# Experts' input rows transposed by VectorE from gathered quarter rows; three waits of the experts' stage moved

## What is computed

```
def swiglu(t, wg, wu, wd):
    return (jax.nn.silu(t @ wg) * (t @ wu)) @ wd

def moe_swiglu(h, router_w, wg, wu, wd):
    ...
    logits = (t @ router_w).astype(jnp.float32)
    top_logits, top_idx = lax.top_k(logits, TOP_K)
    top_w = jax.nn.softmax(top_logits, axis=-1)
    gates = jnp.einsum('tk,tke->te', top_w, jax.nn.one_hot(top_idx, N_EXPERTS, dtype=jnp.float32)).astype(h.dtype)
    y = jnp.zeros_like(t)
    for e in range(N_EXPERTS):
        y = y + gates[:, e:e + 1] * swiglu(t, wg[e], wu[e], wd[e])
    return y.reshape(bsz, s, d)
```

## Time and profile before

| | us |
|---|---|
| median of 3 executions | 1933.41 |
| lowest, highest | 1933.14, 1934.14 |
| the profiled execution's own time | 1928.41 |
| its span, first to last instruction | 1926.7 |

### The profile page before, as it was taken

One profiled execution on the slowest core, in us unless ns is written; L12 is line 12 of the kernel. 1 busy time (PEld: TensorE's weight loads), 2 busy tenths in 40 slices (PEclk: granted clock), 3 DMA queues, 4 the chain that ended last, 5 costly groups with the idle time before them and its releaser, 6 DMA issues. The chain is left out here.

```text
span 1926.7 us, 36862 instructions
## 1 busy us (share of the span) xinstructions
PE 1888.7 (98%) x15078; PEld 1624.8 (84%) x15078; DVE 924.8 (48%) x1225; ACT 578.5 (30%) x1234; POOL 723.9 (38%) x624
## 2 busy tenths in 40 slices
PE   9999999999999999999999999999999999999997
PEld 8778744888887888888877888778999999999996
DVE  3898687667565455444436788865200000000023
ACT  1443213555533111110036657533120211111102
POOL 5755523565544334344526777652200000000011
PEclk9999999999999999999999999999999999999999
DMA  9213750222215666631211111102957578778893
GB/s 336 88 56 143 263 210 34 78 93 88 83 44 202 212 204 213 218 121 61 104 66 67 68 58 69 65 13 83 325 203 251 196 233 275 253 265 333 335 351 152
DMA packets 82824, 313.58 MB, mean 163 GB/s; under 512 B 10121, under 2 KB 10641, under 8 KB 82529
## 3 DMA queue, kind: packets, MB, share of 16 engines
q1 hardware_dynamic: 75952, 289.73, 42.5%
q0 software_dynamic: 4464, 14.35, 2.2%
q10 hardware_dynamic: 2241, 7.14, 1.0%
HBM read 301.43 MB, written 9.75 MB: 162 GB/s over the span
## 5 line engine op out<-in xcount | busy, mean ns | idle before, releaser
L261 PE MATMUL banks<-sb_act,sb_ring 128*64 128x112 f32 (+9 forms) x5088 | 621.0, 300 | 1.1 <-ACT sb_ring L468 0.7
L261 PEld LDWEIGHTS banks<-sb_act,sb_ring 128*128 128x128 f32 (+1 forms) x5088 | 592.5, 174 | 23.1 <-issue 4.5
L261 PE MATMUL banks<-sb_x_norm,sb_ring 128*128 128x256 f32 (+3 forms) x1616 | 330.9, 403 | 3.4 <-ACT sb_ring L468 2.3
L261 PEld LDWEIGHTS banks<-sb_x_norm,sb_ring 128*128 128x128 f32 (+1 forms) x1616 | 242.3, 171 | 66.5 <-issue 29.3
L3732 DVE TENSOR_TENSOR sb_act<-sb_work,banks 128x192 f32<-128x192 f32 (+7 forms) x88 | 27.2, 309 | 482.8 <-PE banks L261 475.2
L443 POOL TENSOR_TENSOR sb_ring<-sb_ring 128x512 f32<-128x512 f32 x146 | 205.1, 1405 | 102.0 <-PE banks L261 53.9
L261 PE MATMUL banks<-sb_work,sb_ring 128*64 128x256 f32 (+2 forms) x1124 | 231.6, 407 | 3.9 <-ACT sb_ring L468 2.7
L261 PEld LDWEIGHTS banks<-sb_work,sb_ring 128*128 128x128 f32 (+1 forms) x1124 | 155.9, 165 | 57.7 <-issue 35.3
L3263 POOL DMA_INDIRECT sb_work<-first_expert_rows,sb_table x8 | 7.5, 939 | 442.6 <-DMA first_expert_rows<-sb_x_norm 440.4
L3534 ACT ACTIVATE sb_work<-banks 128x192 f32<-128x192 f32 (+7 forms) x88 | 25.8, 294 | 295.2 <-PE banks L261 293.2
L2370 ACT ACTIVATE sb_work<-banks 128x256 f32<-128x256 f32 x84 | 32.3, 384 | 216.8 <-PE banks L261 216.8
(11 more groups left out here) (530 smaller groups left out, 2588.8 us busy)
## 6 DMA issues: line engine op xcount, KB each, us to landing
sb_ring<-in_w_moe_up SPq DMA_DIRECT2D x176, 512.0 KB, 4.9
sb_ring<-in_w_moe_down SPq DMA_DIRECT2D x64, 704.0 KB, 6.4
sb_act<-in_cond_w SPq DMA_DIRECT2D x84, 512.0 KB, 3.7
sb_ring<-in_w_ffn_up SPq DMA_DIRECT2D x44, 512.0 KB, 5.2
sb_ring<-in_w_h_in SPq DMA_DIRECT2D x32, 512.0 KB, 4.2
sb_ring<-in_w_in SPq DMA_DIRECT2D x28, 512.0 KB, 5.9
sb_ring<-in_w_m_in SPq DMA_DIRECT2D x24, 512.0 KB, 3.9
sb_ring<-in_w_ffn_down SPq DMA_DIRECT2D x16, 704.0 KB, 5.4
```

The source lines that it names most:

```text
L261: last = m.nc.tensor.matmul(out[part], weights[:, part], act, start=start, stop=stop, skip_group_check=skip)
```

## The change

- Rows in DRAM lie in quarters: `normed_rows` has 2048 rows of 256 values instead of 512 of 1024. A quarter row q holds 32 features of each of the eight blocks of 128. ACT no longer stores them. POOL copies `x_rows` into that order (`quartered`, in `HN` and `more`) after its scatters, once the first gated product of rank 0 is there (`m.evac` at `done + 2`), and stores the copies itself, once weight block 7 of rank 0 has landed.
- The scattered numbers are four times the token. POOL reads them four times, once for each group of 32 partitions, and adds the quarter's number (three small instructions).
- A tile is gathered by four indirect DMAs with 128 quarter rows each: 36 in place of 9.
- DVE transposes a tile with four instructions of 32x32 blocks straight into `xT`, behind the last gated product of a rank. PE's `turn` is gone. ACT's `take_turned` scales and shifts within `xT`.
- `turn_result` stands at the start of the downward blocks of ranks 1 to 5 and no more ahead of block 4, and so does ACT's `take_result`.
- PE starts the downward blocks when ten of the eleven gated blocks are there and waits for the last ahead of its eleventh product.
- ACT waits in rank 0 until the rows are stored, ahead of its copies of the downward blocks.

```diff
self.small = sb("small", [P, 64])
-        self.table = sb("table", [P, 3 * ST + GATHERS + 1 + EXPERTS + 4 * ST], U32)
+        self.table = sb("table", [P, 3 * ST + 1 + EXPERTS + 4 * ST], U32)
+        self.row_parts = sb("row_parts", [P, 4 * GATHERS], U32)
         self.rank_caps = sb("rank_caps", [P, EXPERTS])
...
         self.d_tokens = dram("tokens_of_expert", (PASSES * ROWS, 1), U32)
-        self.d_rows = dram("normed_rows", (S, D))
+        self.d_rows = dram("normed_rows", (4 * S, DG))
         self.d_first = dram("first_expert_rows", (FIRST[-1] + ROWS - sum(CAPS), D))
...
     per_pass = EXPERTS * total
-    over_at = 3 * ST + GATHERS
+    over_at = 3 * ST
     too_many = m.table[0:1, over_at:over_at + 1]
-    token_rows = m.table[:, 3 * ST:3 * ST + GATHERS]
-    tokens = m.d_tokens.rearrange("(p t q) o -> p q (t o)", t=GATHERS, q=P)
+    tokens = m.d_tokens.rearrange("(p g q) o -> p q (g o)", g=4 * GATHERS, q=QUARTER)
+    by_quarter = lambda t: t.rearrange("p (q k c) -> p k q c", q=4, c=QUARTER)
+    stored_rows = m.d_rows.rearrange("(t q) c -> t (q c)", q=4)
+    quartered = [t.rearrange("p a c -> p (a c)") for t in (m.HN[:, 0:2, :], m.HN[:, 2:4, :], m.HN[:, 4:6, :], m.more[:])]
+    row_parted = m.sem("r_row_parted")
     order = m.sem("e_order")
...
                         m.table[:, 2 * ST + t:2 * ST + t + 1], None).then_inc(scattered, 16)
+            pool.wait_ge(m.evac, done + 2)
+            for t in range(ST):
+                pool.wait_ge(row_out, t + 1)
+                give(pool, nc.gpsimd.tensor_copy(by_quarter(quartered[t]), x_rows[:, t, :].rearrange(
+                    "p (k q c) -> p k q c", q=4, c=QUARTER)), row_parted, t + 1)
+            pool.wait_ge(m.loaded[SLOTS - 1], 16 * (uses[SLOTS - 1] + 1))
+            for t in range(ST):
+                pool.dma_start(stored_rows[rows(t, P), :], quartered[t]).then_inc(row_stored, 16)
             pool.wait_ge(scattered, 16 * 2 * ST)
...
                     pool.sem_inc(order, 1)
-                pool.dma_start(token_rows, tokens[p], allow_slow_non_contiguous=True).then_inc(idx_in, 16)
-                pool.wait_ge(idx_in, p * 16 + 16)
+                for q in range(4):
+                    pool.dma_start(m.row_parts[rows(q, QUARTER), :], tokens[p],
+                                   allow_slow_non_contiguous=True).then_inc(idx_in, 16)
+                pool.wait_ge(idx_in, p * 64 + 64)
                 pool.sem_inc(order, 1)
+                for q in range(1, 4):
+                    part = m.row_parts[rows(q, QUARTER), :]
+                    m.glink.on(pool)(nc.gpsimd.tensor_scalar(part, part, q, None, ALU.add))
                 for i in range(first_pass(p), GATHERS):
...
                         pool.sem_inc(order, 1)
-                    nc.gpsimd.indirect_dma_start(
-                        got[i % BUFS], None, m.d_rows,
-                        bass.IndirectOffsetOnAxis(ap=token_rows[:, i:i + 1], axis=0)
-                    ).then_inc(got_sem[i % BUFS], 16)
+                    for q in range(4):
+                        c = 4 * i + q
+                        nc.gpsimd.indirect_dma_start(
+                            got[i % BUFS][:, rows(q, DG)], None, m.d_rows,
+                            bass.IndirectOffsetOnAxis(ap=m.row_parts[:, c:c + 1], axis=0)
+                        ).then_inc(got_sem[i % BUFS], 16)
                 if not first_pass(p):
...
 
-                def turn(i):
-                    pe.wait_ge(got_sem[i % BUFS], p * (16 * got_used[i % BUFS]) + 16 * (
-                        i // BUFS + (i % BUFS > 0) + (not first_pass(p))))
-                    if not first_pass(p) or i >= 3:
-                        pe.wait_ge(turned_out, p * GATHERS + (i - 2))
-                    for k in range(KD):
-                        last = nc.tensor.transpose(ps[:, 4 + 2 * (i % 2) + k // 4, rows(k % 4, P)],
-                                                   got[i % BUFS][:, rows(k, P)], m.c("ident"))
-                    last.then_inc(turned, 1)
-
                 def turn_result(r):
                     pe.wait_ge(m.evac, p * per_pass + (r * total + done + total))
-                    pe.wait_ge(turned_out, p * GATHERS + (need[min(r + 1, EXPERTS - 1)] - 1))
                     for k in range(KD):
...
                     pe.sem_inc(order, 1)
-                    for i in range(need[0]):
-                        turn(i)
                 for r in range(EXPERTS):
...
                         s = b % SLOTS
-                        if b == 4 and 0 < r <= turned_ranks:
-                            turn_result(r - 1)
                         if closing and b >= up:
...
                         if b == up:
+                            if 1 < r <= turned_ranks + 1:
+                                pe.wait_ge(y_copied, p * copies + copies_until(r - 2))
+                                pe.sem_inc(order, 1)
                             if 0 < r <= turned_ranks:
-                                pe.wait_ge(y_copied, p * copies + copies_until(r - 1))
-                                pe.sem_inc(order, 1)
-                            for i in tiles_beside(p, r):
-                                turn(i)
-                            pe.wait_ge(m.evac, p * per_pass + (base + up))
+                                turn_result(r - 1)
+                            pe.wait_ge(m.evac, p * per_pass + (base + up - 2))
                             pe.sem_inc(order, 1)
...
                                 pe.wait_ge(x0_out, max(x0_first, k) + 1)
+                            if b == up and k == KE - 1:
+                                pe.wait_ge(m.evac, p * per_pass + (base + up))
+                                pe.sem_inc(order, 1)
                             if closing and b > up and k == kt // 2:
...
                                                scale=norm.inv[:, t:t + 1]), row_out, t + 1)
-                act.dma_start(m.d_rows[rows(t, P), :], x_rows[:, t, :]).then_inc(row_stored, 16)
             for k in range(KD):
...
                     act.wait_ge(turned, p * GATHERS + i)
-                    pair = 4 + 2 * (i % 2)
                     for k in range(KD):
-                        last = nc.scalar.activation(xT[:, k, rows(i, P)], ps[:, pair + k // 4, rows(k % 4, P)],
-                                                    ACT.Identity, bias=norm.shift(k), scale=norm.scale(k))
+                        x = xT[:, k, rows(i, P)]
+                        last = nc.scalar.activation(x, x, ACT.Identity, bias=norm.shift(k), scale=norm.scale(k))
                     last.then_inc(turned_out, 1)
...
                     for j in range(KE):
-                        if j == 2 and 0 < r <= turned_ranks:
-                            take_result(r - 1)
                         if j == 2 and closing:
...
                                              ACT.Silu).then_inc(silu, 1)
+                    if 0 < r <= turned_ranks:
+                        take_result(r - 1)
                     for i in tiles_beside(p, r):
                         take_turned(i)
+                    if first_pass(p) and r == 0:
+                        act.wait_ge(row_stored, 16 * ST)
                     if closing:
...
             step(nc.vector.tensor_copy(m.table[:, over_at:over_at + 1], most))
-            step(nc.vector.tensor_copy(m.table[:, 2 * ST:3 * ST], m.c("tok_id")))
+            step(nc.vector.tensor_scalar(m.table[:, 2 * ST:3 * ST], m.c("tok_id"), 4.0, None, ALU.mult))
             give(dve, nc.vector.tensor_copy(m.table[:, 0:2 * ST], m.small[:, 3 * ST:5 * ST]), tables, 1)
...
                 for i in (2 * t, 2 * t + 1):
-                    dve.wait_ge(got_sem[i], 16 * ((1 if turn == 1 else PASSES) * got_used[i] - (i == 0) + turn))
+                    dve.wait_ge(got_sem[i], 64 * ((1 if turn == 1 else PASSES) * got_used[i] - (i == 0)) + 16 * turn)
                 a1, a2 = got[2 * t], got[2 * t + 1]
...
 
+            def turn(p, i):
+                dve.wait_ge(got_sem[i % BUFS], p * (64 * got_used[i % BUFS]) + 64 * (
+                    i // BUFS + (i % BUFS > 0) + (not first_pass(p))))
+                for q in range(4):
+                    at = i * P + q * QUARTER
+                    last = nc.vector.transpose(xT[:, :, at:at + QUARTER], got[i % BUFS][:, rows(q, DG)])
+                last.then_inc(turned, 1)
+
             def body(p):
+                if not first_pass(p):
+                    for i in range(need[0]):
+                        turn(p, i)
                 for r in range(EXPERTS):
...
                             mix(j - 4, 1)
+                    for i in tiles_beside(p, r):
+                        turn(p, i)
                     if closing:
...
```

## The result

The changed kernel takes 1956.55 us (median of four, 1954.78 to 1957.73) against 1933.38 (1933.14 to 1934.14) of the kernel before: a ratio of 1.0118, 95% interval 1.0106 to 1.0130. It is **slower** by 23 us; the forecast was 1925.3, faster by 8. In the profiled executions the spans are 1954.1 and 1926.7 us, 27.4 apart.

What follows compares the result with a forecast made beforehand. It took PE to bound the experts' stage, with DMA engines the second limit. Terms -8.15 - 0.3 + 0.3 = -8.15 us gave 1925.3 us; range 1922.8 to 1932.5.

Steps and rivals of the forecast that it cites:

- The step that failed: POOL's queue behind tile 2: the other gathers (36 in all, 45 us) are wanted only in rank 1's downward part; cost 0.
- Transposes off PE: Experts' stage: 72 transposes of gathered tiles leave PE, all on the path; gain 8.15 us.
- VectorE's transposes: Beside downward parts: four DVE transposes a tile, 0.42 us each, hidden while DVE waits for PE; time 0.
- The waits around the downward product: Start after ten of eleven gated blocks: gain 0.3 us in rank 7, cost 0.3 for waits already met.
- Results turned later, ACT in rank 5: Downward part: ACT's first copy needs 8.7 us, four blocks take 9.6; cost 0, upper end 1 us.
- GpSimd's chain: Rank 0: copies, stores, token reads, additions, gathers on POOL; tile 2 lands at 1412, due 1415; cost 0.
- the first rival: Tile 2 lands 1 to 12 us late, PE stands at rank 0's fifth downward block; 1929.3 with 4 us; chance 0.17.
- the doubled chain: Rank 0: slow token reads, copies and landing on GpSimd stall PE by 16 us, 1941 us; chance 0.10.
- GpSimd's wait for the first gate: Rank 0: POOL's copies start only when the first gate ends at 1358.6; no cost of its own.
- the third rival: Ranks 5 to 7: weight loads become the limit as PE asks sooner; half the gain lost, 1929.4 us; chance 0.08.
- The carry to the median: Whole kernel: the profiled execution's 5.0 us under the median was taken to carry over, 1920.3 becoming 1925.3 us.

Runs made afterwards that it cites:

- experiment 9: The repaired kernel, but PE again waits for all eleven gated blocks ahead of a downward part: 1924.56 us, ratio 0.9961.
- the repaired kernel: Changed kernel; GpSimd waits until each tile's four gathers land, rank 7's eight gathers come in two groups of four: 1919.88 us, ratio 0.9936.
- experiment 10: The repaired kernel without GpSimd's wait for the first gated product ahead of its four copies: 1925.46 us, ratio 0.9960.
- experiment 1: Changed kernel with the gathers of tiles 3 to 8 waiting, one tile each, behind every second gated product of rank 1: 1924.68 us.

## Why the prediction was wrong

- **The step that failed** stands at the end of the part on GpSimd's rows: "Queued behind it ... on POOL the other gathers (36 in all, 45 us), wanted only in rank 1's downward part". I counted the gathers and their 45 us, and asked only who waits for them. Their price to all who don't wait for them was put at nothing, and the rows that it rested on show trains of eight. In numbers: 30.0 us in rank 0 (115.87 against 85.83 with the groups apart) and 4.6 in rank 7 (45.21 against 40.66). No rival held this. All that made the kernel slower than forecast were waits for a named thing that comes late, or a gain that isn't there, so the range ended at 1932.5 and the result lies 24 us above it. What the trace of before could have told was the size of the step, four times as many instructions of a kind that had never come in more than eight, and an upper end for that should have reached over the whole train.
- **Transposes off PE** (8.15 us): right. In the kernel with the repaired gathers ranks 0 to 6 are shorter by 1.72, 1.74, 0.99, 0.99, 0.97, 1.30 and 1.16 us, 8.9 together, with the early start in them; without it (experiment 9) they are 6.6 shorter than before, mostly since PE then waits for the last gate in ranks 0 and 6.
- **VectorE's transposes** (0.42 us, ends 0.35 and 0.71): right, 409 ns each, and less when they follow one another, eight in 2.72 us:

```profile
L3737 DVE STREAM_TRANSPOSE sb_act<-sb_work 128x256 f32<-128x256 f32 x36 | 12.5, 409 | 0.0
```

  On the Trainium skill's advice to transpose 128x128 on TensorE where a PSUM destination is fine ("VectorE: DVE Perf Modes", section "Rules for kernel authors"), the measurement decides: with PE the bound and DVE idle, moving 72 of them off PE gave its 8 us once the gathers were in groups.
- **The waits around the downward product** (gain 0.3, cost 0.3, net 0): under-sized. Without the early start the repaired kernel is 3.1 us longer. The reason why I priced it so low was that the transposes had covered the gate; I didn't carry on that, with these gone, the start over ten blocks is what covers it, so that it keeps the other gain from being given back.
- **Results turned later, ACT in rank 5** (cost 0, upper end 1): right. Rank 5 is 1.30 us shorter, no PE wait.
- **GpSimd's chain** was right in its sum and wrong in its parts. In after's timeline:

```profile
1360.63 3.25 POOL L3234 COPY sb_x_norm<-sb_work 128x1024 f32<-128x1024 f32 x3 [3.04 <-DVE sb_act L3750]
...
1365.28 1.68 POOL L3238 DMA_DIRECT2D normed_rows<-sb_x_norm  x3 [0.30 <-POOL sb_more L3234]
...
1381.62 3.44 POOL L3250 DMA_DIRECT2D sb_row_parts<-tokens_of_expert  x4 [14.13 <-issue]
1390.77 1.10 POOL L3256 TENSOR_SCALAR sb_row_parts<-sb_row_parts 32x40 uint32<-32x40 uint32 x3 [5.71 <-DMA sb_row_parts<-tokens_of_expert]
```

  The copies take 1.08 us instead of 1.90, near the lower end, and the issue of four stores 2.2 instead of 5.2. But the last store lands 14.0 us after its issue, not 7, beyond the upper end of 9.4:

```profile
normed_rows<-sb_more POOLq DMA_DIRECT2D x1, 512.0 KB, 14.0
```

  The four reads of token numbers take 9.2 us (forecast 16) and the additions 1.1 (2). So the first gather comes at 1392.2 and the eighth at 1401.2, forecast 1395 and 1404. Tile 2 was in time in every kernel without a stall: the first rival and the doubled chain didn't happen.
- **GpSimd's wait for the first gate** was in the sum only as a start time. It is worth 5 us (experiment 10).
- **Weights**: in the repaired kernel PE waits 0.5 us for a weight block, 0.3 before; the third rival is small.
- **The carry to the median**: before's profiled execution lay 5.0 us under its median; after's, at 1956.02, lies 0.5 under. The difference of medians is 23.2, that of the spans 27.4. As the starts of the stage vary by up to 5 us, a single pair of profiles says no more than that.

## What to carry to other kernels

When a change multiplies the number of indirect DMAs that GpSimd issues in a row, price the train itself, not only who waits for its data: put a group of four or so, then a wait (until they have landed, or for a later step), wherever the data isn't urgent. An "issue" or "remote" wait on several engines at once, with the DMA engines mostly idle and one engine busy at a steady pace, pointed here to that engine and not to a missing semaphore; experiments have to show it. And where a forecast rests on rows of short runs of an instruction, the upper bound for a run four times as long is open.

## What the runs showed of the hardware

- Indirect DMAs of GpSimd that follow one another 1.16 to 1.26 us apart hold up PE, ACT and DVE, at first with late reactions by some tenths of a us to 3 us and more (from about the sixth or seventh on, with gathers of 128 KB), and with PE itself from the tenth to twelfth. Then products start mostly 0.70 us or a multiple of it apart, until 2 to 5 us after the last. Loss in rank 0: 0 us of PE for 8, 11 for 16, 30 for 32 in a row at 1.25 or 1.26 us, 32.6 at 1.16; none at 1.56 or 2.20 us, none for groups of four with waits between them (a later group of eight, in rank 1 of experiment 1, made one gap of 0.65 us), and none for 32 direct DMAs 0.53 us apart.
- The Trainium skill ("SBUF — State Buffer", section "SBUF: two separate sides") says that a DMA can't be slowed by a compute instruction, or the other way round, since their ports are apart. Here indirect DMAs slow all compute engines, and what the runs tie it to is how GpSimd issues them, not their traffic: in the stall the DMA engines were down to 0.33 and 0.25, and 32 direct DMAs of the same bytes stopped nobody at 1.04. No run shows a port as the cause.
- An indirect DMA costs GpSimd nearly the same for 32 rows as for 128: 0.86 and 0.95 us, with 0.30 in between.
